# Final norm of a two-layer decoder step: norm weights and transpositions moved inside the last two output blocks of the last projection, 1/rms applied to rows

## The reference

```python
def rmsnorm(x, g):
    xf = x.astype(jnp.float32)
    y = xf * lax.rsqrt(jnp.mean(xf * xf, axis=-1, keepdims=True) + RMS_EPS)
    return (y * g.astype(jnp.float32)).astype(x.dtype)

def swiglu(h, w_gate, w_up, w_down):
    return (jax.nn.silu(h @ w_gate) * (h @ w_up)) @ w_down
...
    y_prompt = rmsnorm(xp, final_norm)
    y_sample = rmsnorm(xs, final_norm)
```

## Time and profile before

| what | us |
|---|---|
| time, median of 3 runs | 2392.45 (2391.18 to 2393.43) |
| time of the profiled execution | 2392.29 |
| its span | 2390.5 |
| TensorE busy in the span | 2291.4 (96%) |
| DVE busy | 1240.0 (52%) |
| ScalarE busy | 392.4 (16%) |
| GpSimd busy | 1034.5 (43%) |

### The profile page before, as it was taken

One profiled execution on the slowest core, in us unless ns is written; L12 is line 12 of the kernel. 1 busy time (PEld: TensorE's weight loads), 2 busy tenths in 40 slices (PEclk: granted clock), 3 DMA queues, 4 the chain that ended last, 5 costly groups with the idle time before them and its releaser, 6 DMA issues.

```text
span 2390.5 us, 39184 instructions
## 1 busy us (share of the span) xinstructions
PE 2291.4 (96%) x14502; PEld 2055.3 (86%) x14507; DVE 1240.0 (52%) x1723; ACT 392.4 (16%) x853; POOL 1034.5 (43%) x622
## 2 busy tenths in 40 slices
PE   7999999999888999999999999999999899999996
PEld 6999999858565679999999999999986699999996
DVE  5555521579985546555512556542264456555313
ACT  2101000231353312010000110000105420100001
POOL 3546555313001025555555555555550055555552
PEclk9999999999798999999999999999998899999998
DMA  5334463716002433333233333323440023333221
GB/s 129 91 83 102 94 149 80 139 28 148 1 4 84 129 91 77 88 79 82 79 85 85 84 80 87 79 78 84 122 118 10 1 71 80 86 81 81 82 80 52
DMA packets 378102, 196.14 MB, mean 82 GB/s; under 512 B 66563, under 2 KB 374508, under 8 KB 377996
## 3 DMA queue, kind: packets, MB, share of 16 engines
q1 hardware_dynamic: 365532, 178.69, 30.1%
q10 hardware_dynamic: 12128, 15.81, 2.2%
q0 software_dynamic: 352, 0.43, 0.1%
HBM read 191.71 MB, written 11.64 MB: 85 GB/s over the span
## 4 chain that ended last, share of the span: by engine, by line
PE 84%; DVE 7%; ACT 3%; SPq 2%; issue 2%; DMA 1%; POOL 1%; ACTq 0%; DVEq 0%; POOLq 0%
PE psum L540 21%; PE psum L543 14%; PE psum L541 13%; PE psum L539 13%; PE psum L542 11%; PE psum L730 1%; DVE scwA L1635 1%; DVE listsA L1634 1%; DVE XS L1285 1%; DVE nmA L1430 1%; PE psum L696 1%; SPq L400 1%; PE psum L660 1%; PE psum L683 1%; PE psum L759 1%
## 5 line engine op out<-in xcount | busy, mean ns | idle before, releaser
L495 POOL CAST WSP<-WST 128x1024 fp32r<-128x1024 f32 (+1 forms) x305 | 310.5, 1018 | 1163.9 <-PE psum L543 1058.6
L497 POOL TENSOR_TENSOR WSP<-WST,WSP 128x1024 fp32r<-128x1024 f32 (+1 forms) x305 | 722.4, 2369 | 24.4
L540 PE MATMUL psum<-XS,WSP 128*128 128x512 f32 x1672 | 658.3, 394 | 0.0
L539 PE MATMUL psum<-XS,WSP 128*128 128x320 f32 x1672 | 520.4, 311 | 10.4 <-DVE XS L1285 4.3
L543 PE MATMUL psum<-XS,WSP 128*128 128x320 f32 x1672 | 522.3, 312 | 0.0
L541 PE MATMUL psum<-XS,WSP 128*128 128x320 f32 x1672 | 519.0, 310 | 0.0
L542 PE MATMUL psum<-XS,WSP 128*128 128x256 f32 x1672 | 473.7, 283 | 0.0
L542 PEld LDWEIGHTS psum<-XS,WSP 128*128 128x128 f32 x1672 | 314.6, 188 | 71.4
L539 PEld LDWEIGHTS psum<-XS,WSP 128*128 128x128 f32 x1672 | 321.3, 192 | 12.6 <-DVE XS L1285 5.2
L543 PEld LDWEIGHTS psum<-XS,WSP 128*128 128x128 f32 x1672 | 321.2, 192 | 0.0
L540 PEld LDWEIGHTS psum<-XS,WSP 128*128 128x128 f32 x1672 | 314.3, 188 | 0.4
(11 more groups left out here) (295 smaller groups left out, 2706.9 us busy)
## 6 DMA issues: line engine op xcount, KB each, us to landing
WST<-in_ffn_w_gate SPq DMA_DIRECT2D x168, 256.0 KB, 3.8
WST<-in_ffn_w_up SPq DMA_DIRECT2D x168, 256.0 KB, 3.9
WST<-in_ffn_w_down SPq DMA_DIRECT2D x192, 224.0 KB, 3.5
WST<-in_a_w_in SPq DMA_DIRECT2D x28, 256.0 KB, 4.4
kv0A<-in_cache_kv SPq DMA_DIRECT2D x48, 128.0 KB, 2.3
kv2A<-in_cache_kv SPq DMA_DIRECT2D x48, 128.0 KB, 2.2
WST<-in_b_w_in SPq DMA_DIRECT2D x20, 256.0 KB, 4.3
kscr<-in_cache_idx SPq DMA_DIRECT2D x128, 32.0 KB, 2.0
```

Of the source, the lines that this page charges most:

```text
L495: nc.gpsimd.tensor_copy(WSP[s][:, 0, 0:width], WST[s][:, 0:width]).then_inc(w_hi, 1)
L497: nc.gpsimd.tensor_tensor(WSP[s][:, 1, 0:width], WST[s][:, 0:width], WSP[s][:, 0, 0:width].bitcast(F32), ALU.subtract).then_inc(w_split, 1)
L539: mm(front, high, x[:, 0, 0:FRONT], start=first, stop=False)
L540: mm(split, high, x[:, :, FRONT:TOK], start=first, stop=False)
```

## The change

The final norm is computed in another order. The root mean square of a token is one factor for its whole row, so `y = (x * g) * r` is built from `x * g`, transposed, and then scaled by `r` as rows, where `r` is one number for each partition.

- The loop over the down projection of `ffn3` ends after six blocks; blocks 6 and 7 are written out. In the last third (q = 2) of block 6, behind each of the first five `mm3`, TensorE transposes blocks 0 to 3 of one token tile (`y_rows`); in that of block 7, blocks 4 to 6 of one tile. Behind the sixth `mm3` of it, five products with one column of `ones` sum `ssum` (blocks 0 to 6) for each token tile (`token_sums`), with the tokens on partitions.
- ScalarE (`final_update`) scales the blocks 0 to 6 of `X` in place by the norm weight after squaring them, copies the transposed rows to `ytok`, and calls Sqrt once on a constant before the last block's square. `ytok` lies where `XS` is, which is no longer read then.
- The fifth token tile covers tokens 448 to 575, so that its last 64 rows are the sample tokens.
- After the last block: DVE writes the scaled block 7 to `us`; TensorE transposes its five tiles and sums the square of block 7 by five more products; DVE adds both sums into a variance [128, 5], ScalarE takes the root, DVE the reciprocal. DVE scales the rows of tiles 0 to 2 and the last 128 columns of tiles 0 to 3; ScalarE the rows of tiles 3 and 4 and the last columns of tile 4.
- SyncE starts the four stores of the prompt rows, ScalarE that of the sample rows.
- The square of block 7 isn't added to `ssum`, and L1339, L1341, L1795 and the full sum (L560) are not run for the final norm. Two small tensors, `early_sum` and `rtok`, are allocated behind `tail`.

```diff
@@ -228,6 +228,8 @@
         X = sb(ctx, "X", [P, ND, TOK])
+        with ExitStack() as c:
+            ytok = sb(c, "ytok", [P, NTT, D])
         XS = sb(ctx, "XS", [P, 2, ND, TOK], F32R)
@@ -241,6 +243,8 @@
         tail = sb(ctx, "tail", [P, BACK])
+        early_sum = sb(ctx, "early_sum", [P, NTT])
+        rtok = sb(ctx, "rtok", [P, NTT])
         with ExitStack() as c:
@@ -278,6 +282,9 @@
         fin_x, fin_ps, fin_sb = sem("fin_x"), sem("fin_ps"), sem("fin_sb")
+        early_ps, early_set, late_ps, last_ps = sem("early_ps"), sem("early_set"), sem("late_ps"), sem("last_ps")
+        rtok_var, rtok_sd, rtok_set, y_set, y_act = (sem("rtok_var"), sem("rtok_sd"), sem("rtok_set"), sem("y_set"),
+                                                        sem("y_act"))
         kiw_out, kv_out, y_out = sem("kiw_out"), sem("kv_out"), sem("y_out")
@@ -315,6 +322,19 @@
         STAT = PS[3]
+        spare = (at["ffn3"][1] + GU_CHUNKS + 2) % RING
+        Y_BANKS = (bank[2 * spare], bank[2 * spare + 1], bank[6])
+        Y_LAST, Y_SUM = PS[spare], bank[7]
+        def token_tile(t):
+            t0 = min(t * P, TOK - P)
+            return slice(t0, t0 + P)
+        def y_group(k):
+            part, t = divmod(k, NTT)
+            return t, range(0, 4) if part == 0 else range(4, ND - 1)
         def halves(ap):
@@ -472,6 +492,11 @@
             ffn("ffn3", 1, 1)
+            for t in range(NQT):
+                sp.wait_ge(y_set, t + 1)
+                if t >= DVE_ROWS:
+                    sp.wait_ge(y_act, t - DVE_ROWS + 1)
+                sp.dma_start(io["y_prompt"][0, t * P:(t + 1) * P, :], ytok[:, t, :]).then_inc(y_out, 16)
         @block.gpsimd
@@ -585,7 +610,8 @@
                 pe.wait_ge(acc_evac, aend - 1 + RING)
-                with pe.Fori(0, ND // 2) as i:
+                last = name == "ffn3"
+                with pe.Fori(0, ND // 2 - last) as i:
                     for j in range(2):
@@ -596,6 +622,40 @@
                             ins.then_inc(w_used, 1)
+                if not last:
+                    return
+                for d in range(ND - 2, ND):
+                    pe.wait_ge(x_upd, 8 * e + d - 1)
+                    for q in range(RING):
+                        n = n0 + GU_CHUNKS + d * RING + q
+                        pe.wait_ge(w_split, n + 1 + RING)
+                        pe.wait_ge(gh_ready, gh_base(name) + DB * (q + 1))
+                        for b in range(DB):
+                            ins = mm3(aend + d, n % RING, b, P, GS[:, :, q * DB + b, :],
+                                      q == 0 and b == 0, q == RING - 1 and b == DB - 1)
+                            if q == RING - 1 and b < NTT:
+                                y_rows((d - ND + 2) * NTT + b)
+                            if d == ND - 1 and q == RING - 1 and b == NTT:
+                                pe.wait_ge(sq_used, 8 * e + ND - 1)
+                                token_sums(ssum, 0).then_inc(early_ps, 1)
+                        ins.then_inc(w_used, 1)
+            def y_rows(k):
+                t, ds = y_group(k)
+                pe.wait_ge(fin_x, ds[-1] + 1)
+                if k >= len(Y_BANKS):
+                    pe.wait_ge(fin_sb, k - len(Y_BANKS) + 1)
+                for c, d in enumerate(ds):
+                    ins = nc.tensor.transpose(Y_BANKS[k % len(Y_BANKS)][:, c * P:(c + 1) * P], X[:, d, token_tile(t)],
+                                              ident[:, :])
+                ins.then_inc(fin_ps, 1)
+            def token_sums(sums, c0):
+                for t in range(NTT):
+                    ins = mm(Y_SUM[:, c0 + t:c0 + t + 1], sums[:, token_tile(t)], ones[:, 0:1], start=True, stop=True)
+                return ins
             def project_out(name, aend):
@@ -979,19 +1039,13 @@
             ffn("ffn3")
-            pe.wait_ge(x_upd, 8 * 7)
-            statistics(6)
+            pe.wait_ge(fin_x, ND)
+            pe.wait_ge(fin_sb, 2 * NTT)
             for t in range(NTT):
-                w = min(P, TOK - t * P)
-                for h in range(2):
-                    k = 2 * t + h
-                    pe.wait_ge(fin_x, 4 * h + 4)
-                    if k > 2:
-                        pe.wait_ge(fin_sb, k - 2)
-                    for c in range(4):
-                        ins = nc.tensor.transpose(PS[k % 3][0:w, 0, c * P:(c + 1) * P], X[:, 4 * h + c, t * P:t * P + w],
-                                                  ident[:, :])
-                    ins.then_inc(fin_ps, 1)
+                ins = nc.tensor.transpose(Y_LAST[:, t // 4, t % 4 * P:t % 4 * P + P], us[:, token_tile(t)], ident[:, :])
+            ins.then_inc(last_ps, 1)
+            pe.wait_ge(sq_done, 8 * 6 + ND)
+            token_sums(sq, NTT).then_inc(late_ps, 1)
         @block.scalar
@@ -1021,6 +1075,45 @@
                     square(d)
+            def final_update():
+                def square(d):
+                    act.wait_ge(x_upd, 8 * 6 + d + 1)
+                    act.wait_ge(sq_used, 8 * 6 + d)
+                    fn(sq[:, :], X[:, d, :], ACT.Square).then_inc(sq_done, 1)
+                def scaled(d):
+                    act.wait_ge(sq_done, 8 * 6 + d + 1)
+                    fn(X[:, d, :], X[:, d, :], ACT.Copy, scale=gain(6, d)).then_inc(fin_x, 1)
+                def rows(k):
+                    t, ds = y_group(k)
+                    act.wait_ge(fin_ps, k + 1)
+                    fn(ytok[:, t, ds[0] * P:(ds[-1] + 1) * P], Y_BANKS[k % len(Y_BANKS)][:, 0:len(ds) * P], ACT.Copy)\
+                        .then_inc(fin_sb, 1)
+                for d in range(ND - 1):
+                    square(d)
+                    scaled(d)
+                    if d == ND - 3:
+                        for k in range(NTT):
+                            rows(k)
+                for k in range(NTT, 2 * NTT):
+                    rows(k)
+                fn(rtok[:, 0:1], ones[:, 0:1], ACT.Sqrt)
+                square(ND - 1)
+                act.wait_ge(rtok_var, 1)
+                fn(rtok[:, :], rtok[:, :], ACT.Sqrt).then_inc(rtok_sd, 1)
+                act.wait_ge(rtok_set, 1)
+                act.wait_ge(fin_sb, 2 * NTT)
+                for t in range(DVE_ROWS, NTT):
+                    fn(ytok[:, t, 0:D - P], ytok[:, t, 0:D - P], ACT.Copy, scale=rtok[:, t:t + 1]).then_inc(y_act, 1)
+                t = NTT - 1
+                fn(ytok[:, t, D - P:D], Y_LAST[:, t // 4, t % 4 * P:t % 4 * P + P], ACT.Copy, scale=rtok[:, t:t + 1])\
+                    .then_inc(y_act, 1)
+                act.wait_ge(y_act, NTT - DVE_ROWS + 1)
+                act.dma_start(io["y_sample"].rearrange("b t d -> (b t) d"), ytok[P - NS:P, t, :]).then_inc(y_out, 16)
             def root(e):
@@ -1260,18 +1353,7 @@
             ffn("ffn3")
-            update(6)
-            root(6)
-            for t in range(NTT):
-                w = min(P, TOK - t * P)
-                for h in range(2):
-                    k = 2 * t + h
-                    act.wait_ge(fin_ps, k + 1)
-                    fn(xtok[0:w, t, h * SEQ:(h + 1) * SEQ], PS[k % 3][0:w, 0, :], ACT.Copy).then_inc(fin_sb, 1)
-                act.wait_ge(fin_sb, 2 * t + 2)
-                dst = io["y_prompt"][0, t * P:(t + 1) * P, :] if t < NQT else \
-                    io["y_sample"].rearrange("b t d -> (b t) d")
-                act.dma_start(dst, xtok[0:w, t, :]).then_inc(y_out, 16)
+            final_update()
             act.wait_ge(y_out, 16 * NTT)
@@ -1330,7 +1412,11 @@
                         low(e, d)
-                    add_squares(d)
+                    if e < 6 or d < ND - 1:
+                        add_squares(d)
+                    if e == 6 and d == ND - 2:
+                        dve.wait_ge(early_ps, 1)
+                        ts(early_sum[:, :], Y_SUM[:, 0:NTT], 1.0 / D, EPS, ALU.mult, ALU.add).then_inc(early_set, 1)
             def rms(e):
@@ -1790,11 +1876,24 @@
             ffn("ffn3")
-            rms(6)
-            for d in range(ND):
-                stt(X[:, d, :], X[:, d, :], gain(6, d), rstd[:, :], ALU.mult, ALU.mult).then_inc(fin_x, 1)
+            dve.wait_ge(x_upd, 8 * 6 + ND)
+            ts(us[:, :], X[:, ND - 1, :], gain(6, ND - 1), None, ALU.mult).then_inc(fin_x, 1)
+            dve.wait_ge(early_set, 1)
+            dve.wait_ge(late_ps, 1)
+            stt(rtok[:, :], Y_SUM[:, NTT:2 * NTT], 1.0 / D, early_sum[:, :], ALU.mult, ALU.add).then_inc(rtok_var, 1)
+            dve.wait_ge(rtok_sd, 1)
+            nc.vector.reciprocal(rtok[:, :], rtok[:, :]).then_inc(rtok_set, 1)
+            dve.wait_ge(rtok_set, 1)
+            dve.wait_ge(fin_sb, 2 * NTT)
+            dve.wait_ge(last_ps, 1)
+            for t in range(NQT):
+                if t < DVE_ROWS:
+                    ts(ytok[:, t, 0:D - P], ytok[:, t, 0:D - P], rtok[:, t:t + 1], None, ALU.mult)
+                ts(ytok[:, t, D - P:D], Y_LAST[:, t // 4, t % 4 * P:t % 4 * P + P], rtok[:, t:t + 1], None, ALU.mult)\
+                    .then_inc(y_set, 1)
+DVE_ROWS = 3
```

## The result

The changed kernel takes 2379.35 us (median of 5 runs, 2373.43 to 2380.67); the kernel before, timed beside it, 2392.45 us (5 runs, 2390.07 to 2393.43). The ratio is 0.9943, interval 0.9932 to 0.9954: 13.1 us less, where 7.4 were forecast. The time lies 3.15 us under the predicted range. The profiled execution of the changed kernel happens to be the fastest of its five, 2373.43 us with a span of 2371.6, so its span alone overstates the gain.

The account below looks back on a forecast made before the run. TensorE carried 84% of the path, so only the piece behind the last projection could win: 5.85 us of insertions plus a 13.5 us tail, 19.35 against 26.75, 7.4 less, giving 2385.0 us; range 2382.5 to 2388.8.

Parts of the forecast that it names:

- Insertions: 35 transpositions, returns to `mm3` and ten early passes inside blocks 6 and 7: 5.85 us added (4.95 to 9.4).
- Updates, `us`, start of the late transpositions: Behind the last projection: `us` written 1.79 us after E, the five late transpositions starting at 1.94.
- E: End of TensorE's last projection matmul, 2363.75 us in the earlier trace; forecast to move 5.85 us later.
- Ten late passes: TensorE's sums of block 7's square, at full clock from 2.49 us after E, done at 3.7.
- Variance, root, reciprocal: Small operations behind the late passes, 0.2 us each with 0.03 between, done 4.4 us after E.
- C: Rival: Sqrt's table is displaced, two loads of 1.283 us on the path behind E; 2387.6 us, chance 0.04.
- First tile: First token tile of scaled output rows, 1.1 us of scaling, ready for its store 5.5 us after E.
- Stores: Output stores at the end: data from 6.3 us after E, flowing without gaps for 6.2 us.
- A: Rival: the final stores don't close up and need 7.75 us of data; 2386.6 us, chance 0.12.
- Tail: From E to the end of the span: 13.5 us instead of 26.75, bounds 12.7 to 15.05.
- B: Rival: insertions between the `mm3` cost TensorE 9.4 us instead of 5.85; 2388.6 us, chance 0.09.
- D: Rival: mixed-in transpositions and one-column products lower TensorE's clock in blocks 6 and 7; 17 us, 2402 us, chance 0.05.

Follow-up runs that it names:

- e4: The changed kernel unchanged, profiled and timed once more: 2380.54 us.
- f2: The changed kernel with the five transposition groups of blocks 4 to 6 moved behind the last `mm3`: 2377.38 us.
- h3: The changed kernel storing 8 of the 64 sample rows and leaving 56 out: 2380.53 us.
- h1: The changed kernel with the late groups of f2 and `XS` at 64-byte line 547, `WSP` at 1316, `GS` at 1851: 2358.51 us.
- h2: The kernel before with only `XS`, `WSP` and `GS` moved, to 64-byte lines 547, 1316 and 1851: 2368.9 us.
- f3: The changed kernel with all ten transposition groups moved behind the last projection: 2379.21 us.
- e3: The changed kernel with 64 bytes ahead of `XS` and 64 behind it (`XS` at line 547, `WSP` 1316, `GS` 1849): 2369.35 us.
- f1: The changed kernel with `XS` and `GS` both starting 192 bytes past a multiple of 256, `WSP` at line 1318: 2383.75 us.
- f4: The changed kernel with pads putting `XS` at line 548, `WSP` at 1318 and `GS` at 1851.5: 2381.82 us in one execution.
- g2: The kernel of e3 with `GS` at lines 1850, 1851, 1852 and 1853 in ffn0 to ffn3: 2365.6 us in one execution.

## Why the prediction was right and wrong

**What failed.** It is the last sentence of the prediction: the shift of all addresses behind `tail` was named, and set aside with "I found nothing in the rows that depends on these addresses". The rows of one kernel can't show such a dependence when every tensor starts where it starts: all `mm3` of the trace before, on `XS` at 546 and on `GS` at 1846, had the same 0.793, and both differ from `WSP` (1314) by a multiple of four lines. The condition was named for the attention stages; it struck in the down projections, where TensorE is never idle and each nanosecond of a matmul is on the path. Shown by e1 (shift alone, -4.3 us) and e2 (change without shift, 2384.96): the term was put at nothing and measured 4.3 us alone and 5.6 with the change. The difference of the change to e2, 5.6 us, is about what the profile counts in ffn1 to ffn3, 6.15, with ffn0 sometimes beside it. I had no rival of this kind, and "no change before block 6" was wrong for the same reason.

**Step by step**, without the shift the sum was right (-7.5 in e2's profile, -7.4 forecast), with errors in its terms that cancel. That they cancel is luck: 0.9 us less for the insertions stood against 0.8 more for a tail that varies by 1.7 us between profiles.
- Insertions: 5.85 forecast. In e2 blocks 6 and 7 cost 2.20 and 2.72 us over 16.66, so 4.9. A group of four cost 0.43 us: the transpositions start 0.15 behind L568 (2331.52, 2331.67), where L564 would have, L564 0.35 after them, and L565 0.23 after L564 instead of 0.15. Forecast were 0.52, 0.44 for the four and 0.08 for the return. The four do start every 0.11 us, but L564 starts 0.02 behind the fourth, not 0.11. The ten early passes took 1.03 (2354.93 to 2355.96; 1.1 forecast). In the changed kernel the insertions cost a little more: the pitch was 0.780 up to the first transposition of block 6 and 0.793 from there to the end, with `GS` in the same place (so too in e4, f2 and h3). In h1, with `GS` at 1851 and `WSP` at 1316, the same insertions in block 6 left it at 0.780, and block 7 took 17.50 us. The three kernels whose last blocks have none keep 16.38 there (e1, h2, and f3 in block 6). The bound for the low clock was too small: the row of 24 transpositions in 4.33 us spans the clock's rise, and at half clock they start every 0.21 us (e4, 2365.40), not 0.18.
- Updates, `us`, start of the late transpositions: 1.79 and 1.94 behind E forecast, 1.80 and 1.86 measured.
- Ten late passes: "so I take the full rate" failed. The earlier trace rows has 0.81 in 2368:2369, 4.3 to 5.3 us behind E, but that was one execution, with four matmuls (L560) in between; h2, with the same four, had the fall 2.9 us behind E. In the changed kernel the clock was 0.84 in 2359:2360 and 0.50 in 2360:2361, 3 to 4 us behind E, the passes took 1.91 us instead of 1.2, and they ended 4.4 us behind E: 0.7 late. Of nine profiles of this tail only e3 (done at 3.64) and f1 (3.79) were near the 3.7 forecast, three were done at 5.12.
- Variance, root, reciprocal: 0.17, 0.21, 0.19 and the waits between: 0.64 from 2361.48 to 2362.12, 0.7 forecast. The table load (1.28 us, 2354.84) ended 0.9 before E. C did not happen: no load stands behind E.
- First tile 6.1 behind E instead of 5.5, all of it from the passes. SyncE issued the stores 0.03 later.
- Stores: 6.8 us of data instead of 6.2, because of the dip. A forecast 7.75 and gave the 64-partition store as the reason; by h3 it is not the amount of these rows, but their store stays in question. The end came 0.95 behind the last data (1.0).
- Tail: 14.57, and 14.28 in e2, against 13.5, inside the bounds 12.7 to 15.05; e4, f4 and g2 have 15.3 to 15.5, outside them, mostly by the clock (the passes done 1.5 us later than in e3).

**Rivals.** B was refuted by the group above: 0.43 us, not 0.72 at the low-clock price that it assumed (0.85 at the measured one). D did not happen: the clock was 1.00 in both blocks with 35 transpositions and ten passes among the `mm3`. The Trainium skill ("TensorE: Matmul & The Clock Gate", "Part 4: PE-mode transpose") says that a transposition does not count as busy TensorE for the gate in the way a matmul does. In f3 nothing but 40 transpositions and the ten passes ran behind E, for 6.6 us, and the clock fell 9.2 us behind E, where it fell at most 3.9 us behind E in the nine profiles without the extra transpositions. This does not bear the rule out. The same section gives about 275 ns for one 128x128 transposition in a kernel, beside a figure for bfloat16 in isolation; the trace agrees for float32 (0.27 us for a single one), but they start every 0.11 us, and only that counts in a stream.
